# Sink attention in a three-layer block: v held still for pairs of heads, results left turned, inverses turned instead

## The reference, cut to what matters

```python
def one_block(args):            # one block of 128 queries, 256 keys
    q_blk, k_blk, v_blk, blk = args
    valid = band & (blk * BLOCK - BLOCK + kj >= 0)
    s = jnp.einsum('bqhgd,bkhd->bhgqk', q_blk, k_blk) * scale
    s = jnp.where(valid, s, MASK_VALUE)
    m = jnp.maximum(jnp.max(s, axis=-1, keepdims=True), sink)
    p = jnp.exp(s - m)
    p = p / (jnp.sum(p, axis=-1, keepdims=True) + jnp.exp(sink - m))
    return jnp.einsum('bhgqk,bkhd->bqhgd', p, v_blk)
```

## Time and profile before

| | us |
|---|---|
| median of 3 runs (lowest, highest) | 786.54 (785.6, 787.6) |
| the profiled execution's own time | 787.29 |
| its span in the trace | 785.5 |
| TensorE busy in the span | 768.9 |
| VectorE, ScalarE, GpSimd busy | 516.7, 411.1, 231.0 |

### The profile page before, as it was taken

How to read it: one execution, slowest core, us unless ns; L and a number is a source line. 1 busy time by engine, 2 the same in 40 slices (tenths; PEclk the granted TensorE clock), 3 DMA queues, 4 the chain that set the end, 5 groups by cost and what they waited for, 6 DMA issues and landing times.

```text
span 785.5 us, 12585 instructions
## 1 busy us (share of the span) xinstructions
PE 768.9 (98%) x5075; PEld 665.2 (85%) x5075; DVE 516.7 (66%) x759; ACT 411.1 (52%) x662; POOL 231.0 (29%) x186
## 2 busy tenths in 40 slices
PE   8999999999999999999999999999999999999996
PEld 7889987799877889987778888998887888888885
DVE  4846884584556657866557965786678677767453
ACT  5644447634577444344335545718766555456341
POOL 3031896650742000046019910126002111011010
PEclk9999999999999999999999999999999999999999
DMA  9897996377720764655545556440463656655651
GB/s 227 202 244 196 246 214 166 83 181 182 173 83 28 235 174 132 211 189 138 158 134 161 186 191 185 136 135 2 156 216 120 204 173 205 191 184 162 228 174 53
DMA packets 78108, 130.70 MB, mean 166 GB/s; under 512 B 4446, under 2 KB 28242, under 8 KB 77922
## 3 DMA queue, kind: packets, MB, share of 16 engines
q1 hardware_dynamic: 76608, 124.96, 55.5%
q0 software_dynamic: 1200, 4.83, 1.9%
q10 hardware_dynamic: 242, 0.11, 0.0%
HBM read 128.82 MB, written 1.06 MB: 165 GB/s over the span
## 4 chain that ended last, share of the span: by engine, by line
PE 84%; DVE 7%; ACT 3%; DMA 3%; issue 2%; POOL 0%; DVEq 0%; SPq 0%; POOLq 0%; ACTq 0%
PE ps L1554 13%; PE ps L1558 13%; PE ps L1562 13%; PE ps L1594 10%; PE ps L1573 6%; PE ps L1577 6%; PE ps L1581 6%; PE ps L1598 5%; DMA stage<-in_even_w_in 3%; PE ps L1665 2%; DVE w_lo L954 2%; PE ps L1681 1%; ACT w_hi L646 1%; PE ps L1696 1%; PE ps L2037 1%
## 5 line engine op out<-in xcount | busy, mean ns | idle before, releaser
L954 DVE TENSOR_TENSOR w_lo<-stage,w_hi 128x1024 fp32r<-128x1024 f32 x226 | 300.2, 1351 | 157.2 <-ACT w_hi L646 156.7
L646 ACT ACTIVATE w_hi<-stage 128x1024 fp32r<-128x1024 f32 x232 | 242.1, 1061 | 234.3 <-PE ps L1562 108.0
L1554 PE MATMUL ps<-w_hi,act_t 128*128 128x512 f32 (+1 forms) x376 | 102.7, 396 | 2.1 <-ACT w_hi L646 1.6
L1562 PE MATMUL ps<-w_lo,act_t 128*128 128x512 f32 (+1 forms) x376 | 98.8, 385 | 0.1
L1594 PE MATMUL ps<-act_t,w_hi 128*128 128x512 f32 x352 | 88.3, 393 | 0.7 <-DVE act_t L991 0.7
L1554 PEld LDWEIGHTS ps<-w_hi,act_t 128*128 128x128 f32 x376 | 67.8, 188 | 17.6 <-issue 2.8
L1562 PEld LDWEIGHTS ps<-w_lo,act_t 128*128 128x128 f32 x376 | 69.6, 188 | 14.8 <-DVE w_lo L954 0.6
L1558 PE MATMUL ps<-w_hi,act_t 128*128 128x512 f32 (+1 forms) x312 | 81.6, 384 | 0.0
L1594 PEld LDWEIGHTS ps<-act_t,w_hi 128*128 128x128 f32 x352 | 63.3, 189 | 12.2 <-issue 0.9
L1558 PEld LDWEIGHTS ps<-w_hi,act_t 128*128 128x128 f32 x312 | 57.6, 188 | 12.0
L1573 PE MATMUL ps<-act_t,w_hi 128*128 128x256 f32 x416 | 59.0, 284 | 0.6 <-ACT w_hi L646 0.6
(11 more groups left out here) (368 smaller groups left out, 1158.4 us busy)
## 6 DMA issues: line engine op xcount, KB each, us to landing
stage<-in_even_w_in SPq DMA_DIRECT2D x64, 512.0 KB, 5.9
stage<-in_odd_w_in SPq DMA_DIRECT2D x48, 512.0 KB, 4.0
stage<-in_w_gate_up SPq DMA_DIRECT2D x44, 512.0 KB, 4.5
stage<-in_w_down SPq DMA_DIRECT2D x22, 512.0 KB, 4.4
stage<-in_even_w_out SPq DMA_DIRECT2D x16, 512.0 KB, 4.1
stage<-in_odd_w_out SPq DMA_DIRECT2D x16, 512.0 KB, 3.8
stage<-in_w_in SPq DMA_DIRECT2D x10, 512.0 KB, 3.7
stage<-in_w_out SPq DMA_DIRECT2D x8, 512.0 KB, 5.3
```

What stands on the lines that cost most here:

```text
L646: nc.scalar.activation(w_hi[:, u % RING, :], stage[:, u % RING, :], ACT.Copy).then_inc(hi_ready, 1)
L954: nc.vector.tensor_tensor(w_lo[:, u % RING, :], stage[:, u % RING, :], w_hi[:, u % RING, :].bitcast(F32), ALU.subtract).then_inc(lo_ready, 1)
L1554: mm(out[:, b, :], a_hi(k)[:, tok[b]], hi[:, i, :], start=(k == 0), stop=False)
L1562: ins = mm(out[:, b, :], a_hi(k)[:, tok[b]], lo[:, i, :], start=False, stop=(k == k_tiles - 1))
```

## The change

It does the following, in the order of the engines' lists.

- VectorE rotates k ahead of scans 2 and 3; GpSimd's second `rotate_out` waits for the last scan instead of `rope_k_ready`.
- ScalarE makes the upper halves of M0, M1 and G0 between the drains of the q and of the k and v projection, where three such copies stood between the exponentials before. VectorE makes M0's lower half behind the first two heads' maxima, and M1's and G0's at the end.
- The heads go in pairs with `values_of_two`: v stationary, results with channels on the partitions in banks 4 and 5. Odd heads' probabilities are copied back by VectorE (`copy_prob`), even ones by ScalarE.
- The inverse of the sums is needed along the free axis then. VectorE takes the reciprocal of the sums *spread over 64 columns per head* (128 x 512 for each group g of four heads, `inv_wide`), TensorE turns it (8 transposes in all, `turn_inverse`), ScalarE copies it to `inv_t`, and VectorE multiplies (`scale_heads`). The 8 transposes of y_attn go away.
- `mix_attn` 0 needs only group 0 (heads 32 to 35) for its first unit.
- Squares are made on the turned result (ScalarE, 2 x 128 x 512), folded by GpSimd (128 x 512, then 128 x 256), summed over the partitions by two matmuls with a column of ones behind `mix_attn` 0, and copied by VectorE. TensorE waits for that copy ahead of "glu" 1, which writes the same bank.

```diff
@@ gpsimd
                 if ct == 1:
-                    pool.wait_ge(rope_k_ready, 1)
+                    pool.wait_ge(scan_done, CT)
...
+            pool.wait_ge(y_squared, 2)
+            then(nc.gpsimd.tensor_tensor(y_sq[:, 0:2, :], y_sq[:, 0:2, :], y_sq[:, 2:4, :], ALU.add))
+            nc.gpsimd.tensor_tensor(y_sq[:, 0, :], y_sq[:, 0, :], y_sq[:, 1, :], ALU.add).then_inc(y_summed, 1)
             root(4, 512)
@@ scalar
+            split_hi(next_unit[0] + 3)
             chunk_done(act, ("skv", 0))
...
+            copied_behind = {33: 32, 37: 34, 38: 36}
+            for n in range(32, 40):
+                exponentials(n)
+                if n in copied_behind:
+                    copy_prob_act(copied_behind[n])
+                if n in (35, 39):
+                    sink_terms((n - 32) // 4)
+            copy_prob_act(38)
+            for g in range(2):
+                copy_inverse(g)
+            for g in range(2):
+                hi_of_heads(g)
+            for g in range(2):
+                nc.scalar.activation(y_sq[:, 2 * g:2 * g + 2, :], y_t[:, 2 * g:2 * g + 2, :], ACT.Square).then_inc(y_squared, 1)
@@ vector
             ssm_scan(1)
-            ssm_scan(2)
             dve.wait_ge(k_out, 1)
             rope(K_AT, V_AT - K_AT, NB * SINK_H * ROPE_HALF * 4, rope_k_ready)
+            ssm_scan(2)
             ssm_scan(3)
...
+            def invert_sinks(g):
+                dve.wait_ge(sink_exped, g + 1)
+                dve.wait_ge(exped, 36 + 4 * g)
+                n = slice(32 + 4 * g, 36 + 4 * g)
+                then(TT(den[:, :, n], den[:, :, n], sink_exp[:, :, 4 * g:4 * g + 4], ALU.add))
+                nc.vector.reciprocal(inv_wide[:, g].rearrange("p b (h d) -> p b h d", d=HD), den[:, :, n].unsqueeze(3).to_broadcast([P, NB, 4, HD])).then_inc(inv_ready, 1)
+            def scale_heads(g):
+                dve.wait_ge(inv_copied, g + 1)
+                dve.wait_ge(pv_done, 36 + 4 * g)
+                TT(y_t[:, 2 * g:2 * g + 2, :], bank(4 + g).rearrange("p (k n) -> p k n", k=2), inv_t[:, 2 * g:2 * g + 2, :], ALU.mult).then_inc(y_t_ready, 1)
...
+            for i in range(0, 8, 2):
+                score_max(32 + i, 2)
+                score_max(33 + i, 2)
+                if i % 4 == 2:
+                    sink_sums(i // 4)
+                if i >= 2:
+                    copy_prob(32 + i - 1)
+                if i == 0:
                     split_lo(next_unit[0] + 1)
+            for g in range(2):
+                invert_sinks(g)
+            copy_prob(39)
+            scale_heads(0)
+            lo_of_heads(0)
+            scale_heads(1)
+            lo_of_heads(1)
+            split_lo(next_unit[0] + 2)
+            dve.wait_ge(y_sums, 1)
+            nc.vector.tensor_copy(sumsq[:, 8:10], bank(0, NB)).then_inc(squared, NB)
@@ tensor
+            def attend_sinks(q_of, k_of, v_of):
+                for i in range(-2, 10, 2):
+                    n = 32 + i
+                    if i + 2 < 8:
+                        scores_of_pair(n + 2, (q_of(i + 2), q_of(i + 3)), (k_of(i + 2), k_of(i + 3)))
+                    if i == -2:
+                        ssm_lags(2)
+                        ssm_lags(3)
+                    if i == 8:
+                        for g in range(2):
+                            turn_inverse(g)
+                        ssm_states(3)
+                    if i >= 2:
+                        values_of_two(n - 2, v_of)
+                    if i == 2:
+                        ssm_states(1)
+                    if 0 <= i < 8:
+                        turn_prob(n)
+                        turn_prob(n + 1)
+                    if i == 0:
+                        ssm_states(0)
+                    if i == 4:
+                        ssm_states(2)
...
             mix_part("mix_attn", 0, 0, after_lo(3 * KD + 16))
+            pe.wait_ge(y_summed, 1)
+            for b in range(NB):
+                ins = mm(bank(0, 1, b), y_sq[:, 0, b * P:(b + 1) * P], ones[:, 0:1], start=True, stop=True)
+            ins.then_inc(y_sums, 1)
+            pe.wait_ge(squared, squared_count(4))
```

More of the change, by code:

```diff
@@ L234, in build @@
         q_t, k_t = over("q_t", 3072, [P, 4, S]), over("k_t", 4096, [P, KV_H, S])
-        y_attn = over("y_attn", 4608, [P, NB, 512])
+        inv_t, y_t, y_sq = over("inv_t", 3072, [P, 4, S]), over("y_t", 4608, [P, 4, S]), over("y_sq", 0, [P, 4, S])
+        inv_wide = over("inv_wide", 0, [P, 2, NB, 4 * HD])
         gelu_hi, gelu_lo = over("gelu_hi", 5632, [P, CT, S], F32R), over("gelu_lo", 6656, [P, CT, S], F32R)
@@ L281, in build @@
         ret_stats = sem("ret_stats")
-        sink_sum, sink_exped, y_attn_ready = sem("sink_sum"), sem("sink_exped"), sem("y_attn_ready")
+        sink_sum, sink_exped, inv_turned, inv_copied = sem("sink_sum"), sem("sink_exped"), sem("inv_turned"), sem("inv_copied")
+        y_t_ready, y_squared, y_summed, y_sums = sem("y_t_ready"), sem("y_squared"), sem("y_summed"), sem("y_sums")
         sig_ready, ssm_out_ready = sem("sig_ready"), sem("ssm_out_ready")
@@ L339, in copied_by_act @@
         def copied_by_act(n):
-            return n >= FOX_H + DIL_H or n % 16 in COPIED_BY_ACT
+            return n % 2 == 0 if n >= FOX_H + DIL_H else n % 16 in COPIED_BY_ACT
         def wait_copied(eng, n):
@@ L866, in _, with sink_terms, copy_inverse, hi_of_heads @@
             nc.scalar.activation(k_t[:].rearrange("p m n -> p (m n)"), bank(1), ACT.Copy).then_inc(qk_ready, 1)
[L867 to L878, removed]
+            def sink_terms(g):
+                act.wait_ge(sink_sum, g + 1)
+                part = sink_exp[:, :, 4 * g:4 * g + 4]
+                nc.scalar.activation(part, part, ACT.Exp).then_inc(sink_exped, 1)
+            def copy_inverse(g):
+                act.wait_ge(inv_turned, g + 1)
+                nc.scalar.activation(inv_t[:, 2 * g:2 * g + 2, :].rearrange("p k n -> p (k n)"), bank(g), ACT.Copy).then_inc(inv_copied, 1)
+            def hi_of_heads(g):
+                act.wait_ge(y_t_ready, g + 1)
+                for k in range(2 * g, 2 * g + 2):
+                    nc.scalar.activation(act_t[:, k, :], y_t[:, k, :], ACT.Copy, scale=col[:, COL_GATTN + k:COL_GATTN + k + 1]).then_inc(act_hi, 1)
+            copied_behind = {33: 32, 37: 34, 38: 36}
[12 more added lines that the diff above has]
+                nc.scalar.activation(y_sq[:, 2 * g:2 * g + 2, :], y_t[:, 2 * g:2 * g + 2, :], ACT.Square).then_inc(y_squared, 1)
             def take_attn_half(c):
@@ L899, in _ @@
             ahead(("mix_attn", 1))
-            hi_of_turned(3 * KD + 20, 4, 4, COL_GSSM)
+            hi_of_turned(3 * KD + 16, 4, 4, COL_GSSM)
             squares(5, lambda b: ssm_out[:, b, :], lambda b: gate_z[:, b, :])
@@ L909, in _ @@
             ahead(("mix_ssm", 1))
-            hi_of_turned(3 * KD + 24, KD, 0, COL_FFN)
+            hi_of_turned(3 * KD + 20, KD, 0, COL_FFN)
             act.wait_ge(x_ready, 2 * NB)
@@ L1348, in _ @@
             ssm_scan(1)
-            ssm_scan(2)
             dve.wait_ge(k_out, 1)
             rope(K_AT, V_AT - K_AT, NB * SINK_H * ROPE_HALF * 4, rope_k_ready)
+            ssm_scan(2)
             ssm_scan(3)
[L1353 to L1356, removed]
-                    split_lo(next_unit[0] + 1)
-                if i == 8:
-                    dve.wait_ge(scored, 40)
-                    TT(sink_exp[:], neg_max[:, :, 32:40], sink[:].unsqueeze(1).to_broadcast([P, NB, SINK_H]), ALU.add).then_inc(sink_sum, 1)
@@ L1362, in _ @@
[L1362 to L1369, removed]
@@ L1370, in _, with sink_sums @@
-            ins.then_inc(y_attn_ready, 1)
-            lo_of_turned(3 * KD + 16, 4, 0, COL_GATTN, KD)
+            def sink_sums(g):
+                dve.wait_ge(scored, 36 + 4 * g)
+                h = slice(4 * g, 4 * g + 4)
+                TT(sink_exp[:, :, h], neg_max[:, :, 32 + 4 * g:36 + 4 * g], sink[:, h].unsqueeze(1).to_broadcast([P, NB, 4]), ALU.add).then_inc(sink_sum, 1)
+            def invert_sinks(g):
[4 more added lines that the diff above has]
+                nc.vector.reciprocal(inv_wide[:, g].rearrange("p b (h d) -> p b h d", d=HD), den[:, :, n].unsqueeze(3).to_broadcast([P, NB, 4, HD])).then_inc(inv_ready, 1)
@@ new lines, in scale_heads, with lo_of_heads @@
+            def scale_heads(g):
+                dve.wait_ge(inv_copied, g + 1)
+                dve.wait_ge(pv_done, 36 + 4 * g)
+                TT(y_t[:, 2 * g:2 * g + 2, :], bank(4 + g).rearrange("p (k n) -> p k n", k=2), inv_t[:, 2 * g:2 * g + 2, :], ALU.mult).then_inc(y_t_ready, 1)
+            def lo_of_heads(g):
+                for k in range(2 * g, 2 * g + 2):
+                    dve.wait_ge(act_hi, 3 * KD + 16 + k + 1)
+                    STT(act_t[:, KD + k, :], y_t[:, k, :], col[:, COL_GATTN + k:COL_GATTN + k + 1], act_t[:, k, :].bitcast(F32), ALU.mult,
+                        ALU.subtract).then_inc(act_lo, 1)
@@ L1688, in values_of_two @@
                 i = n // 4
-                if n % 4 == 0 and i >= 4:
```

(12 more changed lines are left out.)

## The result

The changed kernel takes 791.46 us (median of 4, 790.38 to 792.24), the kernel before beside it 786.33 (4 runs, 785.6 to 787.6): ratio 1.0061, 95% interval 1.0049 to 1.0072. I had forecast 788.2 with a range of 783.4 to 790.4, and 0.34 for slower. The side was one of the three that I held open, and not the likeliest (0.44 for no change); the size was missed, 5.1 us instead of 1.7.

The account below looks back on a forecast made before the run. TensorE, 98% busy at full clock, was taken as the bound. The glu start moves by (549.4 + 2R - 555.4) + 1.4 = 2R - 4.6, +1.7 us at R = 3.15: 788.2 us beside 786.54, range 783.4 to 790.4.

Parts of the forecast that it names:

- k rotated ahead: Before the scores: rotating k ahead of scans 2 and 3 starts the first scores 0.75 us earlier, nothing lost.
- v held still: Sink heads' values: pairs take 0.80 us each, 3.2 for four against 5.3 for eight single heads; gain 2.1.
- The inverses: End of attention: two wide reciprocals on VectorE hold TensorE, so mix_attn 0 starts at 549.4 + 2R, 555.7 at R = 3.15.
- R: Length of one 128x512 reciprocal on VectorE, taken as 3.15 us; the forecast changes sign at 2.3.
- cheap: Rival at the inverses: R = 0.77 us, glu start 2.6 us earlier, 783.9 us; chance 0.29 for R below 1.
- dear: Rival at the inverses: R = 3.7 to 4.4 us, +2.8 to +4.2, 789.4 to 790.7 us; chance 0.24.
- TensorE's path: From the inverses to mix_attn 0: 546.55 + 0.25 + R + 0.2 + R, then 0.45, states(3) 1.05, values 0.8.
- Squares: Between mix_attn 0 and glu 1: their sums add 1.4 us to TensorE's path, 0.7 of it GpSimd and VectorE taking turns.
- Moved transfers: Weight transfers waiting on later lower halves (M1's at 559 instead of 550.5) stay hidden, with 4 us to spare.
- central case: At the inverses: R near 3.15 us (2.9 to 3.5), 786.9 to 789.3 us with the squares' bounds; chance 0.43.

Follow-up runs that it names:

- e1: The changed kernel with a 128x8 reciprocal per group and a copy spreading it over 128x512; 785.82 us beside 786.82 for the kernel before (0.9991).
- e9: e8 with the squares' column sums in bank 4 and the first group's sink sums behind head 33's copy; 784.07 us beside 786.27 for the kernel before (0.9964).
- e4: The kernel before with four unused reciprocals and four copies, 128x8 to 128x512, on VectorE in the feed-forward; 6.25 ns an element, no kernel time given.
- e2: The changed kernel with 6 and 11 matmuls of ones in TensorE's two waits for the inverses; 789.81 us, ratio 1.0039 to the kernel before.
- e8: e1 with G0's lower half moved behind the first two gelu lower parts; 784.36 us beside 786.56 for the kernel before (0.9971).
- e6: The changed kernel with the squares' column sums moved behind glu 1's first unit; 791.93 us, ratio 1.0064 to the kernel before.
- e7: The changed kernel with the mixer's states(3) ahead of the inverses' turns; 790.11 us, ratio 1.0044 to the kernel before.

## Why the prediction was wrong, step by step

- *k rotated ahead*: right, 0.75 us in the trace of the part alone, at no loss.
- *v held still*: the size of a pair is right (0.65 + 0.22 in the changed chain at 540.47, 0.58 + 0.22 in e1's at 547.32). The "0.50 + 0.19 + 0.39 + 0.19, about 0.9" of a head's exponentials add up to 1.27; the 0.9 stands, since they overlap (two heads begin at 534.79 and 535.68). "Neither ScalarE nor VectorE holds it by more than 0.1" is wrong: VectorE was ready for the inverses 546.32 - 504.48 = 41.84 from the landmark, I had 546.55 - 505.27 = 41.28. That is 0.56 late. Most of it is the stall that the sink sums' 0.98 and the copy of head 33 behind them at 539.78 gave TensorE: with the sums moved in e9, the values of heads 32 and 33 start 0.5 earlier (540.92 - 505.41 = 35.51 from the landmark, where the changed kernel had 35.99).
- *The inverses*: the mechanism was right, R was 3.35 where I took 3.15; den's first addition to the last reciprocal's end took 7.05 and not 6.75, 0.3 too little. The rivals cheap and dear are both refused by R itself and by e4's straight line.
- *The step that failed* is the next: "TensorE's path ... states(3) 1.05, values of 38 and 39 0.8". I priced work behind an idle of 2.8 us at the rate it has in a packed stretch. It took 1.83 + 1.05 + 0.48 = 3.36 instead of 1.85, 1.51 more: the halved clock, shown by e2. (The second turn took 0.15 more than its 0.55, and the mixing starts 0.12 ahead of the values' end, so the step is 1.54 short.) The prediction had read the full clock in the earlier trace rows as a property of the kernel, and gave the idle that it expected no price but its length.
- *Squares*: predicted 1.4 on the path, measured 564.61 - 557.31 = 7.30 from the first mixing to the first glu matmul, before 560.96 - 555.41 = 5.55, so 1.75; 0.35 short, at most 0.1 of it the clock's, which was full again from 557.5. I gave 0.7 to the meeting of GpSimd and VectorE; the additions took 1.69 + 1.60 where alone they take 1.30 + 0.75, and e8 shows that lower halves cause at least the second.
- *Moved transfers*: nothing in the changed trace speaks against it; no experiment tried it.

Sum: 1.7 forecast, + 0.56 + 0.3 + 1.54 + 0.35 = 4.45, beside 4.44 measured from the landmark. The medians differ by 5.1. The 0.7 between is not settled. The two profiled executions differ by 3.8 only, 0.8 of it being the landmark, which the changed kernel's reached earlier. The likeliest source is the slow stretch, whose length varies between executions: 3.4 us in this trace and 6.8 in e6's with the same instructions; the changed kernel's four spans are 788.6 to 790.4 with mean clocks of 0.996 to 0.994, and the profiled one, at 0.996, is on the short side.

The chance of 0.34 for slower was too low and the upper end too near, because no case held a cost that is set by the wait itself. The sum of the central case's own bounds was short too: at R = 3.5, with 2.35 for the squares, it gives 789.9 and not 789.3. With the clock full, e2 measured 789.81, inside the range of 783.4 to 790.4.

## What to carry to other kernels

A stall of TensorE is to be priced with what may follow it at half speed, not by its length alone: here idles of 1.6 and 2.8 us brought 1.5 more, while e1's two waits ahead of glu 1, 1.3 us together, left the clock full. Spread a value after the reciprocal, not before: 0.20 + 0.43 us did what 3.35 had done. When an idle is removed, look what used it as cover: the sums' wait covered the inverse root, and 2.0 us won at glu 1 were gone by ssm_out.

## What the runs showed of the hardware

- VectorE's reciprocal goes by the element, 6.25 ns each over a fixed 0.14 us, at all four widths from 8 to 512.
- A copy on VectorE that spreads one element over 128x512 float32 takes 0.36 us (e4), one that spreads eight 0.43 (e1), less than the 0.686 of a two-input operation of that size with one input in PSUM.
- An addition of 8 columns on VectorE took 0.98 us where it met a GpSimd operation under way, and 0.17 between two of them; one of 16 columns took 0.176 with GpSimd idle.
- TensorE's granted clock fell to 0.50 in the changed kernel at 554.1, 0.7 us after work had come again behind idles of 1.6 and 2.8 us, and stayed there for 3.4 us of work. In e7, and in e6 with the changed kernel's order, it fell during the second idle and stayed for 6.8. With matmuls of ones in both idles (e2) it stayed full.
